# Second and third attention: GpSimd scales the softmax weights, VectorE copies the turned weights

## The chip, the cores and the metric

One core of a Trainium2 chip runs the kernel. TensorE (PE in the rows, its weight loads PEld), VectorE (DVE), ScalarE (ACT), GpSimd (POOL) and SyncE (SP) each run their own list of instructions in order, and wait for one another through semaphores. The metric is the device time of one execution in microseconds.

## The reference

The network is one block with attention over 8 heads and a convolutional feed-forward part, followed by two layers of feed-forward, attention, feed-forward. All is float32, with 256 tokens and a width of 1024. Three attentions occur. In each, per head:

```python
s = einsum(q, k) + bias            # 256 queries x 256 keys, masked to the causal part
m = max(s);  p = exp(s - m)
p = p / sum(p)                     # second attention: a learned sink joins max and sum
out = einsum(p, v)                 # 64 columns of the output per head
```

The second attention (16 heads, a window of 128, keys and values shared by four heads, a sink) and the third (16 heads, causal, a forget gate added to the logits) are the ones that the change touches. The first one (8 heads) is left as it is.

## The kernel before

**Stages.** The list `KINDS` gives eight stages in order: the first attention (`moba`), the convolutional feed-forward (`conv`), a feed-forward, the second attention (`swa`), two feed-forwards, the third attention (`fox`), a feed-forward. All weights come from memory in units of 128x2048 floats through five slots. SyncE issues the loads (L440, L452). Products are made in three passes of a cheaper format: ScalarE rounds each unit to `hi` (L629), VectorE subtracts to get `lo` (L1076), and TensorE multiplies hi by hi, lo by hi and hi by lo. `split_through(s, u)` on either engine means: do this for all units up to unit u of stage s. Where it stands in an engine's list is written out by hand.

**An attention.** The 16 heads go through a pipeline of 19 steps t = 0 to 18, again written out by hand, one loop on each engine. A head's weights are two row blocks: queries 0 to 127 against 128 keys, queries 128 to 255 against 256 keys, so 384 columns in all. There are three buffers for weights (`P_of`, by head modulo 3), two for turned weights (`PT_of`), two banks for logits, one bank at a time for the turned weights. For head h:

- TensorE, step h - 1: `logits` (L1770, L1771), two products. It waits until the maxima of head h - 2 are done.
- VectorE, step h: `max_of` (L1218, L1219) adds the bias, writes the negated logits into the weight buffer and keeps the row extreme. It waits for the logits and until head h - 3 has been turned (its buffer).
- ScalarE, step h: `exps` (L811, L812), exponentials with their sums. In the second attention it waits also for the sink value that GpSimd copies into the buffer (L538, `sinks`).
- VectorE, step h + 1: `normalise` takes the reciprocals of the two sums (L1226), then scales the two blocks (L1228, L1229).
- TensorE, step h + 2: `turn` (L1782), three transposes into a PSUM bank. It waits for the scaled weights and until the bank has been copied out for head h - 1.
- ScalarE, step h + 2: `pt_copy` (L823) copies the bank, 128x384, to SBUF. It stands behind the exponentials of head h + 2.
- TensorE, step h + 3: `values` (L1799, L1800), the product with the values. Two heads share a bank; the first of a pair waits until the pair before has been taken out.
- For each pair ScalarE makes `o_hi` (L829, step h + 3 for an odd head h) and VectorE `o_lo` (L1234, one step later). They stand at the same places in both attentions.

**What else is in the steps.** In VectorE's step the order is: `max_of(t)`, `out_lo` (odd t from 5), `normalise(t-1)`, and then work of the stage: sums and norms of query and key blocks (L1185, L1193, L1200) and `split_through`. In the second attention the splits stand at the end of steps 5, 8, 11, 13 and 15; in the third at the end of steps 0 to 3, 8, 9, 11, 13 and 17. In the third attention step 2 has, after `normalise`: sums of block 4, the split, then the norms of blocks 4 and 5. On TensorE `step_rows` (L1732 to L1734) makes the remaining query, key and value products in the early steps, before `turn`; `turn_block` (L1746) turns normed blocks, and ScalarE's `block_evict` (L783) takes them out. The logits of head 8 wait for the last of these. The output projection `step_out` (L1564 to L1566), 12 matmuls each, follows `values` in TensorE's steps 10, 13, 14 and 17, and after step 18 the rest of it runs, which waits for the last `o_lo`.

**GpSimd.** It sets pads, copies the 16 pairs of sink values in the second attention, and starts loads of modulation weights (L527). After the sinks of the second attention come the loads of the next stages. During the third attention it has no instruction: it waits for the last `values` before its next load.

Of the kernel before, what the change touches and what calls it, by code (L numbers as in the profile page):

```python
# [9 lines left out]
ALU = mybir.AluOpType  # L10
# [118 lines left out]
def build(nc, a, consts, buckets, out):  # L129
    ctx = ExitStack()  # L130
    with ctx:
# [356 lines left out]
        def _(pool):  # L488
# [21 lines left out]
            def load_pieces(stages, most=PIECES * sum(CHUNKS_IN)):  # L510
# [3 lines left out]
                while next_piece < last:  # L514
# [12 lines left out]
                    pool.dma_start(piece_of(n), ada_columns(c)[:, 2 * q:2 * q + 2, :]).then_inc(ada_full[slot], 16)  # L527
                    next_piece += 1

            def sinks(s):  # L530

                pool.wait_ge(nsink_done, 1)
                pool.wait_ge(xt_done, 4 * s + 4)
                for h in range(HEADS[KINDS[s]]):
                    n = HEAD0[s] + h
                    if n >= 3:
                        pool.wait_ge(tr_done, n - 2)
                    nc.gpsimd.tensor_copy(P_of[n % 3][:, P:P + 2 + T:T + 1],  # L538
                                          nsink[:, h:h + 1].to_broadcast([P, 2])).then_inc(sink_set, 1)

            def pad(n, ap, value):

# [70 lines left out]
            load_pieces(6)  # L613
            third_pads(6)
            forget_rows()
            load_pieces(NST)


        @block.scalar
        def _(act):  # L620
# [213 lines left out]

            def attention_outs(s, t):
                nh = HEADS[KINDS[s]]
                if 0 <= t - 2 < nh:
                    pt_copy(s, t - 2)
                if 0 <= t - 3 < nh and (t - 3) % 2:
                    out_hi(s, (t - 3) // 2)  # L840
# [176 lines left out]
        def _(dve):  # L1017
# [204 lines left out]
            def normalise(s, h):  # L1222
                n = HEAD0[s] + h
                st, pr = stat[:, n % 3, :], P_of[n % 3]
                dve.wait_ge(exp_done, n + 1)
                nc.vector.reciprocal(st[:, 4:6], st[:, 4:6]).then_inc(den_ready, 1)  # L1226
                dve.wait_ge(den_ready, n + 1)
                nc.vector.tensor_scalar(pr[:, FIRST], pr[:, FIRST], st[:, 4:5], None, ALU.mult)  # L1228
                nc.vector.tensor_scalar(pr[:, SECOND], pr[:, SECOND], st[:, 5:6], None, ALU.mult).then_inc(nm_done, 1)  # L1229

            def out_lo(s, pair):
                n = HEAD0[s] // 2 + pair
                dve.wait_ge(ohi_done, n + 1)
                nc.vector.tensor_tensor(o_lo[:, pair, :], value_bank(2 * pair), o_hi[:, pair, :].bitcast(F32),  # L1234
                                        ALU.subtract).then_inc(olo_done, 1)

            def attention_step(s, t):
                kind = KINDS[s]
# [5 lines left out]
                    out_lo(s, (t - 5) // 2)  # L1244
                if 0 <= t - 1 < nh:
                    normalise(s, t - 1)
                if t == nh + 2:
                    out_lo(s, nh // 2 - 1)

# [794 lines left out]
```

## Time and profile before

| | us |
|---|---|
| median of 3 runs (lowest, highest) | 1437.64 (1437.03, 1440.68) |
| the profiled execution | 1436.28 |
| its span in the trace | 1434.5 |

| engine | busy us | share of the span |
|---|---|---|
| TensorE, matmuls | 1357.6 | 95% |
| VectorE | 1083.2 | 76% |
| ScalarE | 730.9 | 51% |
| GpSimd | 158.4 | 11% |

The granted TensorE clock is full throughout. The second attention's head pipeline lies between about 642 and 697 us of the span, the third's between about 1144 and 1227 us. A timeline row gives start, duration, engine, line, operation, output <- inputs with shapes, and how many instructions were merged; a bracket at its end gives the idle time of the engine just before it and what ended it. Matmul ends are modelled, so starts are the better thing to subtract.

### The profile page before, as it was taken

The page shows a single profiled execution, that of the slowest core. Times are in us where ns is not written, and L with a number is a line of the kernel's source. Part 1 is how long each engine was busy: PE and PEld are TensorE (multiplying, and loading weights), DVE is VectorE, ACT ScalarE, POOL GpSimd, SP SyncE. Part 2 cuts the span into 40 slices and gives each one's busy share as a digit, 9 for nine tenths or more (in the row PEclk, how much of TensorE's full clock was granted, in tenths as well). Part 3 has the DMA queues.
Part 4 walks back from the last instruction along what each step waited for, and adds up shares of the span by engine and source line. Part 5 has one row for each costly group of instructions (what it writes and reads, how often), then busy time and mean ns, then how long its engine had stood idle before and what let it go on. Part 6 is the DMA issues. An engine that isn't in the chain of part 4 may idle for free.

```text
span 1434.5 us, 18439 instructions
## 1 busy us (share of the span) xinstructions
PE 1357.6 (95%) x7209; PEld 1154.7 (80%) x7209; DVE 1083.2 (76%) x1506; ACT 730.9 (51%) x1023; POOL 158.4 (11%) x230
## 2 busy tenths in 40 slices
PE   2899999999989999997999999999999998999998
PEld 1699988999968888786788887788887877788886
DVE  5888976999888999667678888688887656675444
ACT  3664464444564333677643345634437867743432
POOL 1111000111001221000011113011101000100000
PEclk9999999999999999999999999999999999999999
DMA  9877755888759998441588896698874531585561
GB/s 351 284 232 258 237 191 186 296 287 293 255 161 356 337 354 297 166 151 59 176 276 307 293 297 235 208 315 308 296 251 147 172 124 62 188 279 178 176 201 62
DMA packets 188794, 333.57 MB, mean 233 GB/s; under 512 B 8434, under 2 KB 131966, under 8 KB 187684
## 3 DMA queue, kind: packets, MB, share of 16 engines
q1 hardware_dynamic: 161392, 236.02, 48.9%
q0 software_dynamic: 26736, 96.14, 19.6%
q8 instruction: 58, 0.95, 0.3%
q10 hardware_dynamic: 580, 0.23, 0.1%
q14 instruction: 28, 0.23, 0.0%
HBM read 331.24 MB, written 1.12 MB: 232 GB/s over the span
## 4 chain that ended last, share of the span: by engine, by line
PE 76%; DVE 11%; ACT 6%; issue 4%; DMA 3%; SPq 0%; ACTq 0%; DVEq 0%
PE bank L1601 10%; PE bank L1603 10%; PE bank L1602 10%; PE bank L1564 8%; PE bank L1566 7%; PE bank L1565 7%; PE bank L1496 4%; PE bank L1497 4%; PE bank L1498 4%; DVE lo L1076 4%; DVE ada_sum L1034 2%; ACT hi L629 2%; PE bank L1732 2%; PE bank L1734 2%; PE bank L1733 2%
## 5 line engine op out<-in xcount | busy, mean ns | idle before, releaser
L1076 DVE TENSOR_TENSOR lo<-raw,hi 128x2048 fp32r<-128x2048 f32 x215 | 490.8, 2287 | 89.2 <-ACT hi L629 88.7
L629 ACT ACTIVATE hi<-raw 128x2048 fp32r<-128x2048 f32 x215 | 405.7, 1910 | 19.2 <-DMA raw<-in_w_out 12.3
L1601 PE MATMUL bank<-hi,h_hi 128*128 128x512 f32 x704 | 278.1, 395 | 3.6 <-DVE lo L1076 2.0
L1603 PE MATMUL bank<-hi,h_lo 128*128 128x512 f32 x704 | 274.5, 390 | 0.0
L1602 PE MATMUL bank<-lo,h_hi 128*128 128x512 f32 x704 | 274.2, 389 | 0.0
L1564 PE MATMUL bank<-hi,o_hi 128*128 128x512 f32 x504 | 203.5, 404 | 11.1 <-DVE lo L1076 9.0
L1566 PE MATMUL bank<-hi,o_lo 128*128 128x512 f32 x504 | 197.2, 391 | 0.0
L1565 PE MATMUL bank<-lo,o_hi 128*128 128x512 f32 x504 | 196.6, 390 | 0.0
L741 ACT ACTIVATE KT<-bank 128x256 f32<-128x256 f32 x88 | 33.8, 384 | 313.4 <-PE bank L1603 313.4
L1601 PEld LDWEIGHTS bank<-hi,h_hi 128*128 128x128 f32 x704 | 132.2, 188 | 33.4 <-DVE lo L1076 3.9
L1603 PEld LDWEIGHTS bank<-hi,h_lo 128*128 128x128 f32 x704 | 132.2, 188 | 28.1
L1602 PEld LDWEIGHTS bank<-lo,h_hi 128*128 128x128 f32 x704 | 132.3, 188 | 26.2
L1496 PE MATMUL bank<-h_hi,hi 128*128 128x256 f32 x480 | 137.9, 287 | 3.3 <-DVE lo L1076 3.2
L1498 PE MATMUL bank<-h_hi,lo 128*128 128x256 f32 x480 | 135.7, 283 | 0.0
L1497 PE MATMUL bank<-h_lo,hi 128*128 128x256 f32 x480 | 135.7, 283 | 0.0
L527 POOL DMA_DIRECT2D ada<-in_ada_w x100 | 71.3, 714 | 523.3 <-DVE ada_sum L1034 396.5
L1034 DVE SCALAR_TENSOR_TENSOR ada_sum<-ada,c_act,ada_sum 128x512 f32<-128x512 f32 x156 | 117.1, 750 | 8.8 <-DMA ada<-in_ada_w 2.2
L1564 PEld LDWEIGHTS bank<-hi,o_hi 128*128 128x128 f32 x504 | 94.8, 188 | 31.8 <-DVE lo L1076 12.3
L1034 DVE SCALAR_TENSOR_TENSOR ada_sum<-V,c_act,ada_sum 128x512 f32<-128x512 f32 x152 | 113.9, 749 | 3.9
L1566 PEld LDWEIGHTS bank<-hi,o_lo 128*128 128x128 f32 x504 | 94.6, 188 | 20.7
L1565 PEld LDWEIGHTS bank<-lo,o_hi 128*128 128x128 f32 x504 | 95.0, 188 | 17.4
L1165 DVE TENSOR_TENSOR KT<-KT,bank 128x256 f32<-128x256 f32 x88 | 36.2, 417 | 83.1 <-ACT KT L741 83.1
(217 smaller groups left out, 1993.9 us busy)
## 6 DMA issues: line engine op xcount, KB each, us to landing
raw<-in_ffn_w SPq DMA_DIRECT2D x176, 512.0 KB, 5.3
ada<-in_ada_w POOLq DMA_DIRECT2D x100, 512.0 KB, 5.9
raw<-in_ffn_w SPq DMA_DIRECT2D x44, 1024.0 KB, 6.3
V<-in_ada_w POOLq DMA_DIRECT2D x76, 512.0 KB, 6.1
raw<-in_w_up SPq DMA_DIRECT2D x22, 1024.0 KB, 6.4
raw<-in_w_in SPq DMA_DIRECT2D x16, 1024.0 KB, 7.9
raw<-in_fox_w_in SPq DMA_DIRECT2D x12, 1024.0 KB, 5.1
raw<-in_w_down SPq DMA_DIRECT2D x11, 1024.0 KB, 5.2
```

Source lines behind the costliest of these rows:

```text
L629: nc.scalar.activation(hi[:, n % NS, :], raw[:, n % NS, :], ACT.Copy).then_inc(hi_ready, 1)
L1034: nc.vector.scalar_tensor_tensor(acc, in0=src, scalar=c_act[:, col:col + 1], in1=acc, op0=ALU.mult, op1=ALU.add).then_inc(ada_step, 1)
L1076: nc.vector.tensor_tensor(lo[:, n % NS, :], raw[:, n % NS, :], hi[:, n % NS, :].bitcast(F32), ALU.subtract).then_inc(lo_ready, 1)
L1496: mm(outp, wh, xh, start=start, stop=False, skip_group_check=True)
L1497: mm(outp, wh, xl, start=False, stop=False, skip_group_check=True)
L1498: return mm(outp, wl, xh, start=False, stop=stop, skip_group_check=True)
L1564: mm(outp, xk_hi, wh[:, k, cut], start=start, stop=False, skip_group_check=True)
L1565: mm(outp, xk_hi, wl[:, k, cut], start=False, stop=False, skip_group_check=True)
L1566: ins = mm(outp, xk_lo, wh[:, k, cut], start=False, stop=stop, skip_group_check=True)
L1601: mm(bank[:, :], xk_hi, wh[:, i, :], start=k == 0, stop=False, skip_group_check=True)
L1602: mm(bank[:, :], xk_hi, wl[:, i, :], start=False, stop=False, skip_group_check=True)
L1603: ins = mm(bank[:, :], xk_lo, wh[:, i, :], start=False, stop=k == KD - 1, skip_group_check=True)
```

## The change

In the stages other than the first (`if s`), three things change:

- `normalise` on VectorE ends after the reciprocals. GpSimd gets a new function `weights`, which waits for them and scales the two blocks in two instructions. In the second attention it is called for head h - 1 behind the sink copy of head h; in the third for heads 0 to 15 behind `forget_rows`, before the next loads.
- ScalarE no longer copies the turned weights (`pt_copy` only for `s == 0`).
- VectorE gets `turned_weights(s, t - 2)`, at the end of its `attention_step(t)`, behind the reciprocals of head t - 1 and ahead of the block work and splits of the step. It waits for the turn of head t - 2 and for the `values` of head t - 4, then copies 128x384 from the bank.

```diff
+            def weights(s, h):
+                n = HEAD0[s] + h
+                st, pr = stat[:, n % 3, :], P_of[n % 3]
+                pool.wait_ge(den_ready, n + 1)
+                nc.gpsimd.tensor_scalar(pr[:, FIRST], pr[:, FIRST], st[:, 4:5], None, ALU.mult)
+                nc.gpsimd.tensor_scalar(pr[:, SECOND], pr[:, SECOND], st[:, 5:6], None, ALU.mult).then_inc(nm_done, 1)
...
@@ def sinks(s), in the loop over h, and behind it
+                    if h:
+                        weights(s, h - 1)
+                weights(s, HEADS[KINDS[s]] - 1)
...
             forget_rows()
+            for h in range(HEADS["fox"]):
+                weights(6, h)
             load_pieces(NST)
...
             def attention_outs(s, t):
                 nh = HEADS[KINDS[s]]
-                if 0 <= t - 2 < nh:
+                if 0 <= t - 2 < nh and s == 0:
                     pt_copy(s, t - 2)
...
                 nc.vector.reciprocal(st[:, 4:6], st[:, 4:6]).then_inc(den_ready, 1)
+                if s:
+                    return
                 dve.wait_ge(den_ready, n + 1)
...
+            def turned_weights(s, h):
+                n = HEAD0[s] + h
+                dve.wait_ge(tr_done, n + 1)
+                dve.wait_ge(pv_done, n - 1)
+                dst = PT_of[n % 2].rearrange("p (a b) -> p a b", a=3)
+                if KINDS[s] != "fox":
+                    dst = dst[:, :, ::-1]
+                nc.vector.tensor_copy(dst, turn_bank(h)[:, 0:384].rearrange("p (a b) -> p a b", a=3)).then_inc(ptc_done, 1)
...
                     normalise(s, t - 1)
+                if s and 0 <= t - 2 < nh:
+                    turned_weights(s, t - 2)
                 if t == nh + 2:
                     out_lo(s, nh // 2 - 1)
```

## Rows read from the trace of the kernel before

**Rows 1.** The page, part 1: busy us, share, instructions of each engine.

```profile
PE 1357.6 (95%) x7209; PEld 1154.7 (80%) x7209; DVE 1083.2 (76%) x1506; ACT 730.9 (51%) x1023; POOL 158.4 (11%) x230
```

**Rows 2.** Busy time by stretch: PE, PEld, DVE, ACT, POOL, clock, DMA share, GB/s.

```profile
650.00:697.30 47.30, 37.96 (x218) 31.17 (x216) 34.74 (x112) 35.50 (x88) 5.46 (x16) 1.00 0.24 76
1186.40:1227.00 40.60, 35.52 (x186) 28.92 (x187) 25.23 (x74) 27.55 (x63) 0.56 (x1) 1.00 0.24 78
```

**Rows 3.** Waits of PE, second attention: us in total, times, longest.

```profile
PE bank L1782 <- ACT work L823: 3.4, 3, 2.4
```

**Rows 4.** Waits of PE, third attention.

```profile
PE bank L1782 <- ACT work L823: 1.7, 3, 1.0
PE bank L1782 <- issue: 1.5, 1, 1.5
```

**Rows 5.** Groups of instructions, whole span: count, busy us, mean ns, idle before.

```profile
L823 ACT ACTIVATE work<-bank 128x384 f32<-128x384 f32 x40 | 19.2, 481 | 13.8 <-PE bank L1782 13.7
...
L1057 DVE TENSOR_REDUCE modc<-bank 128x4 f32<-128x512 f32 x44 | 30.1, 683 | 1.7 <-PE bank L1532 1.7
...
L1234 DVE TENSOR_TENSOR o_lo<-bank,o_hi 128x256 fp32r<-128x256 f32 x20 | 8.5, 423 | 21.6 <-ACT o_hi L829 21.5
```

**Rows 6.** GpSimd's compute instructions: duration ns min/median/max, starts, forms.

```profile
L545 POOL MEMSET VP<- x6: 317/532/536, 60.4 to 1109.9; 128x512 f32 x4, 128x256 f32 x2
L538 POOL COPY work<-nsink x16: 187/189/795, 623.1 to 685.4; 128x2 f32<-128x2 f32 x16
```

**Rows 7.** Timeline, second attention, PE.

```profile
649.87 0.49 PE L1782 MATMUL bank<-ident,work 128*128 128x128 f32 x3
...
676.43 0.49 PE L1782 MATMUL bank<-ident,work 128*128 128x128 f32 x3
...
679.95 0.52 PE L1782 MATMUL bank<-ident,work 128*128 128x128 f32 x3
680.68 0.67 PE L1799 MATMUL bank<-work,VP 128*128 128x256 f32 x2 [0.21 <-DVE o_lo L1234]
...
688.57 0.49 PE L1782 MATMUL bank<-ident,work 128*128 128x128 f32 x3
...
691.39 0.55 PE L1782 MATMUL bank<-ident,work 128*128 128x128 f32 x3 [0.47 <-DVE work L1229]
```

**Rows 8.** Timeline, second attention, DVE.

```profile
650.51 0.35 DVE L1218 CUSTOM_DVE_ANT_0 work<-bank,TB,nsink 128x128 f32<-128x128 f32 x1 [3.11 <-PE bank L1782]
...
675.44 2.29 DVE L1076 TENSOR_TENSOR lo<-raw,hi 128x2048 fp32r<-128x2048 f32 x1 [0.72 <-ACT hi L629]
677.65 0.34 DVE L1218 CUSTOM_DVE_ANT_0 work<-bank,TB,nsink 128x128 f32<-128x128 f32 x1
...
678.33 0.16 DVE L1226 RECIPROCAL stat<-stat 128x2 f32<-128x2 f32 x1
...
690.59 0.16 DVE L1226 RECIPROCAL stat<-stat 128x2 f32<-128x2 f32 x1
```

**Rows 9.** Timeline, second attention, POOL.

```profile
676.99 0.80 POOL L538 COPY work<-nsink 128x2 f32<-128x2 f32 x1 [4.21 <-PE bank L1782]
```

**Rows 10.** Timeline, third attention, PE.

```profile
1159.80 0.49 PE L1782 MATMUL bank<-ident,work 128*128 128x128 f32 x3
...
1186.37 0.46 PE L1770 MATMUL bank<-TB,q_rows 128*128 128x128 f32 x2 [1.54 <-issue]
...
1217.49 0.49 PE L1782 MATMUL bank<-ident,work 128*128 128x128 f32 x3
...
1220.83 0.52 PE L1782 MATMUL bank<-ident,work 128*128 128x128 f32 x3 [1.00 <-ACT work L823]
```

**Rows 11.** Timeline, third attention, DVE.

```profile
1162.78 0.69 DVE L1200 TENSOR_TENSOR std<-bank,hstd 128x512 f32<-128x512 f32 x1
...
1215.73 0.15 DVE L1226 RECIPROCAL stat<-stat 128x2 f32<-128x2 f32 x1
...
1216.38 0.16 DVE L1226 RECIPROCAL stat<-stat 128x2 f32<-128x2 f32 x1
```

## The prediction

> **What bounds the kernel now.** I read the page first: TensorE's matmuls fill 95% of the span, VectorE 76%, ScalarE 51% [rows 1]. Then the busy time by stretch. In the second attention from 650 us on TensorE is busy 37.96 of 47.3 us, so some 9 us are open, with VectorE at 34.74 and ScalarE at 35.50; in the third from 1186.4 on, 35.52 of 40.6, so 5 us are open [rows 2]. The change can win or lose only there. Third, the waits of TensorE: the turn (L1782) of a head waits for ScalarE's copy of the head before, three times and 3.4 us in the second attention [rows 3], three times and 1.7 us in the third, and a further turn waits 1.5 us that the view gives to no one, behind the same copy [rows 4]. Those 6.6 us are the most that moving the copy off ScalarE gives. Last, the timelines of TensorE and VectorE, step against step, which decide where the copy lands.
>
> **ScalarE's part.** It loses 32 copies of 0.48 us [rows 5], 15.4 us. It bounds no stage, so this is worth only what starts earlier behind it.
>
> **VectorE's own work.** The slot of reciprocals and two scalings is 0.65 us, from one reciprocal to the next (1215.73 to 1216.38) [rows 11]. Without the scalings and the wait for the reciprocals I leave 0.12. The copy is new here: from PSUM a reduction over 512 columns takes 0.68, a subtraction over 256 takes 0.42 [rows 5], so 384 columns take 0.55 by interpolation, 0.47 from start to start. 0.12 + 0.47 = 0.59 against 0.65: nothing won or lost. Bounds 0.42 and 0.68.
>
> **GpSimd's part.** No row shows arithmetic on this engine. Its copy of two columns takes 0.19, its memset 0.53 for 512 columns and 0.32 for 256 [rows 6], so 0.83 ns per column. Below: memset's rate for both blocks, 0.5 us. For reading and writing one after the other: 2 x 384 x 0.83 ns + 2 x 0.19 = 1.0 us. Above: twice that, 2.1. I take 1.1, near the middle row. From reciprocal to turn is 0.80 us today (690.59 to 691.39) [rows 7, 8]; less 0.5 for VectorE's scalings, plus 1.1, plus 0.1 for one more hop between engines makes 1.5 us. The Trainium skill, GPSIMD Engine Reference, "Performance versus the Vector engine", gives 1.8 cycles per element at 1.2 GHz for a tight loop; with two fixed parts of 0.19 an estimate from it is 0.96 us, and the sum below would be 0.3 us less. The same page's "Engine selection" advises VectorE for elementwise work, which speaks against the move.
>
> **The new wait, which carries the forecast.** VectorE now waits, in step t, until TensorE has turned head t - 2. Behind the waiting copy stand, in order, the step's block work, its `lo` split of 2.2 us, the next maximum and the next reciprocals. TensorE turns head t - 2 late in step t where something long precedes it. A reader of the bank starts 0.63 us after the turn starts (649.87, 650.51) [rows 7, 8]. I went through both attentions head by head; four places matter.
>
> 1. Second attention, step 11. `step_out` of step 10 holds the turn of head 9 until 676.43 [rows 7]. Today VectorE's split begins at 675.44 and the next maximum at 677.65 [rows 8]. Afterwards: 676.43 + 0.63 + 0.47 = 677.53, split until 679.74. The maximum takes 0.68 to the reciprocals (677.65 to 678.33) [rows 8], then 1.5: head 11 is turned at 681.9 where it was turned at 679.95, +2.0. The product with values behind it lay 0.73 after the turn today, waiting for `o_lo` (680.68) [rows 7], and needs only 0.33; so +1.6 reaches `step_out` of step 13 and everything behind it.
> 2. Second attention, step 15. `step_out` of step 14 holds the turn of head 13. Today VectorE's split is over at 690.59 when TensorE has just passed that turn at 688.57, and the last turn comes 2.82 us after it, at 691.39 [rows 7, 8]. Afterwards the chain is turn, 0.63, copy 0.47, split 2.2, reciprocals of head 15, 1.5: 4.8 us. +2.0. The last `step_out`s wait for this head.
> 3. Third attention, step 2. Seven products a step keep the turn of head 0 until 1159.80 [rows 10]. VectorE's order behind it is copy (until 1160.9), sums 0.6, split 2.2, norm: the norm of block 4 starts at 1164.0 and not at 1162.78 [rows 11], and TensorE's next product waits for it, +1.2. The head pipeline later waits for ScalarE's evictions: 1.54 us before the logits of head 8 (1186.37) [rows 10]. ScalarE lost five copies by then, so I cost this at 0. If that cover failed it would be +1.2.
> 4. Third attention, end. There is no split at step 15. Head 13 is turned at 1217.49, then 0.63 + 0.47, reciprocals of head 15 at 1218.6, and 1.5: 1220.1. Today the last turn is at 1220.83, because the copy before it stood behind a rounding on ScalarE [rows 10]. -0.7.
>
> The 6.6 us of waits on ScalarE's copy go, but at steps 4 to 10 what is late next is `o_lo` behind VectorE's own list, or the evictions, within 0.2 us of today's times. **Sum:** +1.6 + 2.0 + 0 - 0.7 = +2.9 us. Against the profiled execution's 1436.28 us that is 1439.2; that run is 1.36 us below the median of the runs, so the median becomes 1437.64 + 2.9 = 1440.5 us. GpSimd's bounds enter at three places (turns of heads 11 and 15, then 15): -1.8 and +3.0. So the forecast's own range is +1.1 to +5.9, 1438.7 to 1443.5.
>
> **The shared port.** Can GpSimd work beside the splits? A sink copy of two columns that takes 0.19 took 0.80 (676.99 to 677.79), and the split beside it began at 675.44 with 2.29 us, so ended at 677.73 [rows 8, 9]. GpSimd waited for the split's end. The Trainium skill, SBUF — State Buffer, "Who interferes with whom", says the pair of ports is an exclusive lock, and that whichever starts first holds it for the whole instruction. By that rule the trace agrees for GpSimd as the loser; no row shows VectorE as the loser. In the forecast GpSimd begins right after the reciprocals, while VectorE still copies, so it comes first and the split waits up to 0.6 us at steps 5 and 8 of the second attention and 9 and 11 of the third. Those delays lie before longer waits and are within the 0.2 above.
>
> **The rivals.**
> - *Locked out or slow GpSimd.* The second scaling meets a running split and ends 2.2 us later, or the two take 2.1 us. With 1.0 more at each of three places the time is +2.9 + 3.0 = +5.9; one turn behind a split (head 8 of the third attention, where today's wait of 1.5 leaves 0.9 uncovered) adds 1.3 to +2.9. I give +5, 1442.6 us. For: the 0.80 us copy. Against: the order of starts. 0.22.
> - *ScalarE's relief carries* (the other side). The roundings `hi` come up to 1 us earlier, the turns wait for no one, and VectorE's copy finds its turn done. Then of 6.6 us some 2.0 stay as new waits on `o_lo`: -4.6, 1433.0 us. It decides where TensorE has passed the turn of head t - 2 when VectorE reaches the copy. Against: at steps 11 and 15 of the second attention it has not, by 1.0 us and more. 0.10.
> - *No change.* The work moves but the losses at steps 11 and 15 are made up, because heads before them run about 2 us earlier than I have them and TensorE reaches `step_out` sooner. 1437.6 us. 0.18.
> - *The forecast*, +2.9: 0.50.
>
> **How the numbers follow.** Runs of this kernel tell a difference from none at about 0.3%, 4.3 us. Of the forecast's 0.50 about 0.36 lie within that and 0.14 above; of the locked-out case 0.05 within and 0.17 above; the relief case halves into 0.05 faster and 0.05 within; no change gives 0.18. Faster 0.05, same 0.64, slower 0.31. The range: leaving out the larger gains and the worst GpSimd gives 1434.5 to 1445.5.
>
> **What would show it.** In the changed profile: (a) VectorE's copy waits for L1782, over 2 us in all, longest at steps 11 and 15 of the second attention; (b) ScalarE falls by 15 us and VectorE stays within 3; (c) the last turn of the second attention falls 3 to 4 us after today's 691.39, the last of the third half a microsecond earlier relative to its start; (d) GpSimd's two scalings together near 1.1 us, the ones that meet a split longer; (e) the stages outside the two attentions have the same lengths. Wrong would be: no wait of VectorE on turns with a shorter second attention, or GpSimd's scalings beyond 2 us.

## The result, and the profile after

| | before | after |
|---|---|---|
| median of the runs (lowest, highest), us | 1437.61 (1437.03, 1440.68) | 1449.99 (1448.34, 1451.24) |
| span of the profiled execution | 1434.5 | 1449.4 |
| TensorE clock over the span | 0.996 | 0.987 |

The change makes the kernel slower by 12.4 us between the medians; the ratio is 1.0081 with a 95% interval of 1.0067 to 1.0096, which is 11.6 us. Four executions of the kernel after were measured, and 4 to 12 of each kernel below; ratios leave out one, of *scaling alone*, that took 7149 us. The prediction was 1440.5 us with a range up to 1445.5: right in the sign of its shift, far too small, and the time is outside the range.

The line numbers moved: the turn L1782 is L1808, `values` L1799 is L1825, the logits L1770 are L1796, `o_lo` L1234 is L1249, the split L1076 is L1089. GpSimd's scalings are L535 and L536, its sink copy L546, VectorE's copy L1259. Part 1 of the page of the kernel after, against [rows 1]:

```profile
PE 1368.2 (94%) x7209; PEld 1163.0 (80%) x7209; DVE 1080.7 (75%) x1474; ACT 719.3 (50%) x991; POOL 211.5 (15%) x294
```

VectorE has lost 2.5 us, ScalarE 11.6, GpSimd has gained 53.1. TensorE has the same instructions and is busy 10.6 us longer. That is the first sign that something other than waiting has been added.

Where the 14.9 us between the two profiled executions lie, read as start times on TensorE. A length here is the time from the first logits of an attention to the first `step_out` product behind its last head; it is used for all kernels below.

| stretch | before | after | difference |
|---|---|---|---|
| up to the first logits of the second attention | 641.74 | 642.69 | +0.95 |
| second attention | 55.52 | 65.74 | +10.22 |
| between | 446.22 | 446.21 | 0 |
| third attention | 83.40 | 87.09 | +3.69 |
| the rest of the span | 207.6 | 207.7 | +0.1 |

Busy time by stretch of the kernel after (columns as in [rows 2]), first over both attentions, then the places with a reduced clock:

```profile
641.00:700.00 59.00, 49.10 (x241) 39.66 (x240) 36.23 (x112) 33.82 (x85) 28.57 (x45) 0.88 0.15 49
700.00:712.00 12.00, 9.62 (x39) 7.97 (x40) 3.27 (x7) 4.17 (x5) 4.19 (x6) 0.86 0.58 185
1145.00:1245.00 100.00, 90.50 (x444) 74.55 (x443) 54.87 (x133) 61.62 (x115) 28.98 (x36) 0.97 0.31 106
...
660.00:670.00 10.00, 8.16 (x29) 6.42 (x28) 4.97 (x19) 5.90 (x15) 5.78 (x9) 0.50 0.00 0
671.00:677.00 6.00, 3.66 (x23) 2.86 (x22) 4.96 (x14) 1.78 (x7) 2.42 (x6) 1.00 0.00 0
686.00:692.00 6.00, 5.44 (x20) 4.52 (x21) 4.12 (x11) 3.78 (x10) 5.11 (x7) 0.72 0.00 0
700.00:706.00 6.00, 4.64 (x17) 3.97 (x18) 1.04 (x3) 1.91 (x1) 2.75 (x4) 0.72 0.70 231
```

The granted clock was 1.00 in both stretches of [rows 2]. It was not full throughout the span of the kernel before, contrary to what stands above: from 38 to 45 us and near 217 us it was at the lower level, both far from the two attentions. The second of these places:

```profile
215.00:220.00 5.00, 4.63 (x26) 4.63 (x27) 3.73 (x4) 2.82 (x4) 0.00 (x0) 0.66 0.00 0
```

In the kernel after the clock is 0.88 over the second attention: TensorE runs at the lower of its two levels, 1.2 GHz, from 660 to 670 us, near 688 and near 702, and twice in the third attention. Each time a pause of TensorE stands before the fall or around it; but the pause before 675 us, 2.3 us long and the reason for the low busy time in the row from 671 us, is followed by no fall. The waits of TensorE (as in [rows 3]) in the second attention, then VectorE's on the turn, second and third attention:

```profile
PE bank L1808 <- POOL work L536: 4.8, 4, 2.6
PE bank L1825 <- DVE o_lo L1249: 4.2, 2, 2.3
```

```profile
DVE work L1259 <- PE bank L1808: 19.8, 11, 3.6
...
DVE work L1259 <- PE bank L1808: 25.0, 12, 5.0
```

ScalarE's copy is gone from TensorE's list, as it was meant to be. In its place stand GpSimd's scaling and `o_lo`, and VectorE stands before the turn for 44.8 us in all.

The timeline of the kernel after, TensorE, at the two places of the second attention that the forecast was built on, and at the first fall of the clock:

```profile
656.17 0.55 PE L1808 MATMUL bank<-ident,work 128*128 128x128 f32 x3
658.61 0.67 PE L1825 MATMUL bank<-work,VP 128*128 128x256 f32 x2 [1.90 <-DVE o_lo L1249]
...
660.00 1.06 PE L1797 MATMUL bank<-KT,QT 128*128 128x256 f32 x2
662.03 0.90 PE L1808 MATMUL bank<-ident,work 128*128 128x128 f32 x3 [0.97 <-POOL work L536]
...
680.86 0.49 PE L1808 MATMUL bank<-ident,work 128*128 128x128 f32 x3
...
686.56 0.55 PE L1808 MATMUL bank<-ident,work 128*128 128x128 f32 x3 [0.76 <-POOL work L536]
...
696.34 0.49 PE L1808 MATMUL bank<-ident,work 128*128 128x128 f32 x3
...
701.36 0.90 PE L1808 MATMUL bank<-ident,work 128*128 128x128 f32 x3 [2.61 <-POOL work L536]
```

From the turn of head 9 to that of head 11 it is 5.70 us, where it was 3.52 [rows 7]; from head 13 to head 15, 5.02 for 2.82. A turn takes 0.5 us at the full clock and 0.90 at the lower one. The first fall lies between two pauses: TensorE has waited 1.90 us before 658.61, its products are slow from 660.00 on (1.06 us for two logits, 0.60 at the full clock), and the wait of 0.97 us that ends at 662.03 is already inside the slow stretch. VectorE and GpSimd in the same two neighbourhoods:

```profile
658.91 2.28 DVE L1089 TENSOR_TENSOR lo<-raw,hi 128x2048 fp32r<-128x2048 f32 x1
...
696.87 0.56 DVE L1259 COPY work<-bank 128x384 f32<-128x384 f32 x1 [2.12 <-PE bank L1808]
697.34 2.28 DVE L1089 TENSOR_TENSOR lo<-raw,hi 128x2048 fp32r<-128x2048 f32 x1
699.54 0.16 DVE L1239 RECIPROCAL stat<-stat 128x2 f32<-128x2 f32 x1
```

```profile
658.63 0.60 POOL L535 TENSOR_SCALAR work<-work,stat 128x128 f32<-128x128 f32 x1 [2.39 <-DVE stat L1239]
659.21 2.77 POOL L536 TENSOR_SCALAR work<-work,stat 128x256 f32<-128x256 f32 x1
...
699.79 0.60 POOL L535 TENSOR_SCALAR work<-work,stat 128x128 f32<-128x128 f32 x1 [3.43 <-DVE stat L1239]
700.37 0.93 POOL L536 TENSOR_SCALAR work<-work,stat 128x256 f32<-128x256 f32 x1
```

The chain at step 15 is link for link that of the forecast: turn, copy, split, reciprocals, scaling, turn. At 659.21 GpSimd's second scaling takes 2.77 us and not 0.93, because a split has started at 658.91; it ends 0.8 us behind that split. Over the whole span (durations in ns, least, median and most, as in [rows 6]):

```profile
L535 POOL TENSOR_SCALAR work<-work,stat x32: 596/606/610, 646.4 to 1234.2; 128x128 f32<-128x128 f32 x32
L536 POOL TENSOR_SCALAR work<-work,stat x32: 916/927/2770, 647.0 to 1234.8; 128x256 f32<-128x256 f32 x32
L546 POOL COPY work<-nsink x16: 177/188/2095, 624.1 to 693.1; 128x2 f32<-128x2 f32 x16
```

### The profile page after: what moved, and what is told of

It is laid out like the page before. It is cut to its first block, busy times and chain, and to the rows that moved or that the text cites. A ratio compares the mean times of both kernels' runs of the same rounds, so it can differ in the third digit from the quotient of the medians.

```text
span 1449.4 us, 18441 instructions
## 1 busy us (share of the span) xinstructions
PE 1368.2 (94%) x7209; PEld 1163.0 (80%) x7209; DVE 1080.7 (75%) x1474; ACT 719.3 (50%) x991; POOL 211.5 (15%) x294
## 4 chain that ended last, share of the span: by engine, by line
PE 77%; DVE 11%; ACT 4%; issue 3%; DMA 3%; POOL 1%; SPq 0%; ACTq 0%; DVEq 0%
PE bank L1627 10%; PE bank L1629 10%; PE bank L1628 10%; PE bank L1590 8%; PE bank L1592 8%; PE bank L1591 8%; PE bank L1522 4%; PE bank L1523 4%; PE bank L1524 4%; DVE lo L1089 3%; DVE ada_sum L1047 2%; PE bank L1758 2%; PE bank L1760 2%; PE bank L1759 2%; PE bank L1638 1%
## 5 line engine op out<-in xcount | busy, mean ns | idle before, releaser
L1089 DVE TENSOR_TENSOR lo<-raw,hi 128x2048 fp32r<-128x2048 f32 x215 | 490.8, 2286 | 82.4 <-ACT hi L642 82.1
L527 POOL DMA_DIRECT2D V<-in_ada_w x76 | 54.6, 719 | 369.6 <-DVE ada_sum L1047 364.4
```

What stands on the lines that cost most here:

```text
L1089: nc.vector.tensor_tensor(lo[:, n % NS, :], raw[:, n % NS, :], hi[:, n % NS, :].bitcast(F32), ALU.subtract).then_inc(lo_ready, 1)
```

## The experiments

Theory A: VectorE's wait for the turn, in order ahead of its block work and splits, carries the loss. Theory B: GpSimd does, by its latency and its lock-outs. Theory C: the pauses take TensorE's clock to 1.2 GHz, and that multiplies whatever A or B cost. Where a cost is given "by the ratio", it is the ratio's distance from 1 times the median before. Ratios are to the kernel before, run in the same rounds; its median over those runs was 1438.4 to 1438.6, and 1437.61 beside the kernel after. The lengths and clocks are those of one profiled execution each.

| kernel | median us | ratio (95%) | second | third | clock, span |
|---|---|---|---|---|---|
| before | 1438.55 | | 55.52 | 83.40 | 0.996 |
| after | 1449.99 | 1.0081 (1.0067, 1.0096) | 65.74 | 87.09 | 0.987 |
| copy alone | 1445.41 | 1.0057 (1.0039, 1.0075) | 61.10 | 85.14 | 0.992 |
| scaling alone | 1439.25 | 1.0007 (0.9997, 1.0018) | 56.99 | 83.40 | 0.993 |
| copy last | 1439.49 | 1.0011 (1.0000, 1.0022) | 57.18 | 82.98 | 0.997 |
| splits wait | 1445.72 | 1.0059 (1.0040, 1.0078) | 62.17 | 85.00 | 0.991 |
| fillers | 1445.37 | 1.0055 (1.0034, 1.0077) | 60.55 | 85.55 | 0.999 |
| copy last, VectorE scales | 1440.53 | 1.0015 (1.0003, 1.0026) | 58.05 | 82.16 | 0.998 |
| two splits ahead | 1445.35 | 1.0045 (1.0032, 1.0057) | 57.38 | 85.46 | 0.996 |
| outs first | 1438.18 | 1.0001 (0.9988, 1.0014) | 56.21 | 83.45 | 0.996 |
| before with fillers | 1439.53 | 1.0011 (1.0002, 1.0020) | 57.54 | 83.63 | 0.998 |
| third alone | 1439.83 | 1.0015 (1.0003, 1.0028) | 56.18 | 85.44 | 0.996 |
| third, copy last, VectorE scales | 1436.57 | 0.9987 (0.9977, 0.9997) | 55.53 | 82.21 | 0.998 |
| six places late | 1443.75 | 1.0037 (1.0022, 1.0051) | 62.01 | 83.70 | 0.990 |

**Each half by itself.** *Copy alone*: VectorE scales as before and copies as in the change.

```diff
@@ normalise, against the kernel after
-                if s:
-                    return
@@ sinks, and behind forget_rows: the calls of weights are gone
```

> Only the copy is moved: VectorE scales as before and copies the turned weights at the place of the change; ScalarE has no copy, GpSimd no scaling. The whole change costs +12.4 us. Theory A (VectorE's in-order wait for the turn carries the loss): +3 to +6 us. Theory B (GpSimd's latency of 1.53 us between reciprocal and turn, and its lock-out by the splits, carry it): -1 to +2 us. Theory C (TensorE's pauses drop its clock, and the clock carries most of it): no long pause of TensorE is left here, so the granted clock of the second attention is back near 1.00 and the time within 2 us of A's or B's.

*Scaling alone*: GpSimd scales, ScalarE copies.

```diff
@@ attention_outs on ScalarE, against the kernel after
-                if 0 <= t - 2 < nh and s == 0:
+                if 0 <= t - 2 < nh:
@@ attention_step on VectorE
-                if s and 0 <= t - 2 < nh:
-                    turned_weights(s, t - 2)
```

> Only the scaling is moved: GpSimd scales, ScalarE copies the turned weights as before. Theory A: +1 to +3 us, since no engine waits for a turn ahead of a split. Theory B: +7 to +11 us. Theory C: the loss follows the granted clock of the second attention (0.88 in the changed kernel): if it stays under 0.93 the loss is over +5 us, if it is above 0.98 under +3 us.

By the ratios the copy alone costs 8.2 us (7.0 by the medians), more than A expected (+3 to +6), and the scaling alone 1.0, at the low end of it. B falls: its +7 to +11 for the scaling does not come, and GpSimd's extra latency lengthens the second attention by 1.5 us and the third not at all. The two halves add up to 9.2 us of the 11.6 by the ratios, a difference that the intervals leave open; the lengths of the two attentions, one profiled execution each, add up to 8.8 of 13.9. C's expectation for the copy alone, no long pause and a clock near 1.00, failed. TensorE waits there 2.38 and 2.46 us for `o_lo`, and its clock falls twice in the second attention, so these 8 us hold a share of the clock as well:

```profile
642.36:703.46 61.10, 49.74 (x257) 41.04 (x256) 45.85 (x147) 34.85 (x87) 6.40 (x16) 0.94 0.21 69
```

**The same copy at another place.** *Copy last*: the whole change, but each step of VectorE ends with the copy, behind the block work and the split.

```diff
@@ attention_step on VectorE, against the kernel after
-                if s and 0 <= t - 2 < nh:
-                    turned_weights(s, t - 2)
@@ the loops of the second and the third attention, last in the step
+                        if 0 <= t - 2 < HEADS[kind]:
+                            turned_weights(s, t - 2)
```

> The whole change, but VectorE's copy stands at the very end of each step, behind the block work and the split of the step. A split no longer waits for a turn. Theory A: the copies are later by a split in five steps, but the splits and maxima are back; +6 to +9 us instead of +12.4. Theory B: nothing gained, +11 to +14 us, since GpSimd then starts beside the split at every split and is locked out five times in each attention.

Ten of the 11.6 us go by the ratios, 11.3 of the 12.4 by the medians, more than both theories expected, with the same instructions on every engine. Waits of VectorE on the turn in that kernel, second and third attention:

```profile
DVE work L1259 <- PE bank L1810: 7.5, 6, 3.6
...
DVE work L1259 <- PE bank L1810: 9.7, 7, 3.2
```

19.8 and 25.0 us have become 7.5 and 9.7, and what is left has no split behind it in its own step. So the order in VectorE's list is the cause. That the copy runs on VectorE is not. The clock stayed full in this kernel's second attention, so what the order and what the clock gave back come together here. GpSimd's scaling was locked out by a split three times in it (2.56, 2.66 and 2.56 us for 0.60), against twice in the kernel after, so the lock-outs by themselves cannot carry the loss:

```profile
L535 POOL TENSOR_SCALAR work<-work,stat x32: 594/603/2658, 647.1 to 1222.4; 128x128 f32<-128x128 f32 x32
```

**The lock-outs.** *Splits wait*: the whole change, and a split of an attention step starts only when the scaling of that step is done.

```diff
@@ the loop of the second attention on VectorE; in the third likewise
                         if t in (5, 8, 11, 13, 15):
+                            dve.wait_ge(nm_done, HEAD0[s] + t)
                             split_through(s, 6 + (5, 8, 11, 13, 15).index(t))
```

> The whole change, and before each split of steps 5, 8, 11, 13, 15 (second attention) and 8, 9, 11, 13, 17 (third) VectorE also waits until GpSimd has scaled, so no scaling is locked out. The two lock-outs of 1.84 us (a scaling of 2.77 instead of 0.93) go, each split there is up to 1.3 us later. Theory A: no change, +11 to +13.5 us. Theory B with the lock as its main part: +8 to +10 us, and the clock of the second attention above 0.92.

4.3 us come back by the medians and 3.2 by the ratios, whose intervals overlap with those of the kernel after. The loss left is 8.5 us by the ratio, as the lock theory expected, and 7.3 by the medians, a little under it. In the second attention head 4 is turned 17.75 us after the first logits, and 19.34 in the kernel after, where its scaling takes 2.77. TensorE's clock falls here too, at other places (1.00 from 660 to 670 us, 0.83 from 670 to 680), so the time of this run does not separate lock-out and clock. The traces do in part. *Two splits ahead*, below, has the lock-out and a full clock, and this kernel's clock is full as well until just before the turn of head 8. Head 4 is turned at 19.35 us there and at 17.75 here, but head 5 at 22.59 and 23.19, and head 8 at 30.45 and 31.68. In the second attention, then, the lock-out costs nothing that lasts to head 5, and making the split wait costs 1.2 us by head 8; what this run wins over the kernel after comes with a shorter and later fall of the clock. In the third attention the lock-out does cost: head 8 is turned at 57.26 us here, although the clock has just fallen, and at 58.47 with the change in the third alone, at the full clock.

**The clock by itself.** *Fillers*: the whole change, nothing taken away, and 43 products of the identity with itself whose output nothing reads, where the kernel after pauses.

```diff
@@ TensorE, against the kernel after
+            FILL_TURN = {("swa", 4): 4, ("swa", 15): 10, ("swa", 11): 3, ("fox", 11): 3}
+            FILL_VALUES = {("swa", 2): 7, ("swa", 6): 8, ("fox", 8): 8}
+            def filler(bank, count):
+                for _ in range(count):
+                    mm(bank[:, 0:P], ident[:, :], ident[:, :], start=True, stop=True)
@@ turn and values: filler(...) behind the wait for ptc_done, ahead of the wait for nm_done or olo_done
```

> The changed kernel with products of the identity with itself put where its trace has TensorE waiting over half a microsecond: in the second attention before the values of heads 2 and 6 and the turns of heads 4, 11 and 15, in the third before the values of head 8 and the turn of head 11; 43 products that nothing reads, in banks that are free there. Work is added and nothing taken away, no edge between engines is changed. Theory C (the pauses drop TensorE's clock to 1.2 GHz and that multiplies the loss): the granted clock of the second attention goes back from 0.88 to over 0.97, and the time falls although there is more to do: the stretches at half speed in the changed kernel cost some 7 us in the second attention and 3.5 in the third by their busy time, of which I expect 4 to 8 us back, so 1442 to 1446. Rival (the clock is a bystander): the time stays at 1449 to 1452 or rises with each filler that overshoots its pause, whatever the clock does.

```profile
641.00:700.00 59.00, 53.33 (x321) 45.25 (x319) 37.24 (x114) 35.31 (x86) 32.76 (x48) 1.00 0.21 65
700.00:712.00 12.00, 10.98 (x50) 8.96 (x49) 5.45 (x7) 5.86 (x12) 1.44 (x2) 1.00 0.52 177
1145.00:1245.00 100.00, 91.02 (x476) 76.19 (x474) 57.00 (x133) 60.99 (x119) 28.89 (x36) 1.00 0.36 122
```

The clock is 1.00 throughout (same stretches as above), and the kernel is faster for doing more, by 4.6 us between the medians and 3.7 between the ratios (four executions each; the two intervals overlap by 0.001). One filler group overshoots, as TensorE's and GpSimd's rows at step 15 show (a product of the identity counts as two instructions):

```profile
696.01 2.50 PE L1805 MATMUL bank<-ident 128*128 128x128 f32 x20 [1.52 <-DVE work L1259]
698.35 0.49 PE L1817 MATMUL bank<-ident,work 128*128 128x128 f32 x3
```

```profile
696.18 0.92 POOL L536 TENSOR_SCALAR work<-work,stat 128x256 f32<-128x256 f32 x1
```

The scaling ends at 697.10, the turn starts at 698.35: about 1.2 us too many. *Before with fillers* is the control: the same 43 products in the kernel before.

> Control of the run with fillers: the kernel before with the same 43 products of the identity at the same seven places. Its clock is at full speed there and its pauses lie elsewhere, so there is nothing to win back. Theory C (fillers helped the changed kernel only by its clock): slower than the kernel before, by +2 to +8 us (43 products of 0.25 us are 10.8 us, part of which falls in pauses that exist here too). Rival (filler products shorten something by themselves): 1438 or less.

It is 1.0 us slower by the medians and 1.6 by the ratio. That is less than the 2 I expected at least, since more of the products fall in pauses than I had counted; but they win nothing where the clock is full. Theory C holds; the two kernels compared at the end of the next part say the same without fillers.

**Which places.** *Two splits ahead*: only the two steps that the forecast charged.

```diff
@@ attention_step on VectorE, against the kernel after
+                if kind == "swa" and t in (11, 15):
+                    split_through(s, 6 + (5, 8, 11, 13, 15).index(t))
                 if s and 0 <= t - 2 < nh:
                     turned_weights(s, t - 2)
```

> The changed kernel with the splits of steps 11 and 15 of the second attention put ahead of the copy, all other steps as in the change. These are the two places that the prediction charged, 1.6 and 2.0 us. Theory A as predicted (these two places hold the whole loss): 1438 to 1440. Theory A widened (the in-order wait costs at every step that has a split, and each pause is doubled by the clock): the turns of the changed kernel are already 5.7 us late at head 11, so only the later half comes back, 4 to 6 us: 1444 to 1446.

*Third alone*: the change only where `KINDS[s] == "fox"`.

> The change in the third attention alone; the second is as in the kernel before. The third attention took 3.7 us longer in the changed kernel, 2.15 with its clock at full speed in the run with fillers. Theory A with C: +2 to +4 us in all, 1440.5 to 1442.5, with the stall at the turned block of step 2 (1.0 us) in the trace. Rival (the loss in the third is carried over from the second): within 1 us of the kernel before.

2.2 us by the ratio, 1.3 by the medians, a little under what I expected; the third attention takes 85.44 us, +2.0, and the stall at the turned block is there with 1.02. The loss in the third is its own and not carried over. The second attention of this kernel is that of the kernel before, instruction for instruction, and the clock fell in it all the same, from 658.8 to 662.2 us: it took 56.18 us for 55.52. The stretch from 655 to 665 us:

```profile
655.00:665.00 10.00, 6.91 (x35) 5.88 (x36) 7.97 (x27) 7.32 (x25) 0.40 (x3) 0.83 0.00 0
```

*Six places late*: the copy stands behind block work and split at six steps.

```diff
@@ against the kernel after
+            LATE = {"moba": (), "swa": (11, 15), "fox": (2, 4, 9, 11)}
-                if s and 0 <= t - 2 < nh:
+                if s and 0 <= t - 2 < nh and t not in LATE[kind]:
                     turned_weights(s, t - 2)
@@ the loops of the second and the third attention, last in the step
+                        if t in LATE[kind]:
+                            turned_weights(s, t - 2)
```

> The changed kernel with VectorE's copy moved behind the block work and the splits at six of its 38 steps only: steps 11 and 15 of the second attention, steps 2, 4, 9 and 11 of the third. Theory A with places: these six carry nearly all of the loss, so the second attention takes 57 to 58 us (55.5 before, 65.7 after), the third 83 to 84 (83.4 and 87.1), and the whole is +1.5 to +4 us, 1440 to 1442. Rival (the wait at every step adds up): over 1445.

The whole is +5.3 us by the ratio, above the 1.5 to 4 expected and under the rival's 1445. In the third attention the six-places kernel is back at 83.70, from 85.44 with the change in the third alone, but that does not show that the loss sat at steps 2, 4, 9 and 11. Head 5 is turned at 44.91 us, 46.34 with the change in the third alone, so the later copies of steps 2 and 4 give back 1.4 us. The pauses of TensorE before the `values` of head 6 and the turn of head 8 stay, 2.19 and 1.99 us, because the copy of step 8 still stands ahead of its split. In the second, *two splits ahead* and *six places late* have the same order on every engine, yet one took 57.38 us and the other 62.01. Busy time from 10 to 20 and from 20 to 30 us after the first logits, first of *two splits ahead*, then of *six places late*:

```profile
656.54:666.54 10.00, 6.24 (x39) 4.68 (x38) 8.71 (x26) 7.20 (x20) 7.32 (x11) 1.00 0.30 100
666.54:676.54 10.00, 6.84 (x44) 5.63 (x43) 8.12 (x27) 6.61 (x19) 7.04 (x10) 1.00 0.00 0
```

```profile
652.45:662.45 10.00, 6.77 (x37) 4.91 (x36) 8.64 (x25) 7.20 (x20) 7.32 (x11) 0.86 0.29 97
662.45:672.45 10.00, 8.95 (x39) 7.37 (x37) 4.82 (x15) 5.63 (x15) 4.35 (x8) 0.63 0.00 0
```

VectorE, ScalarE and GpSimd do the same in the first of the two stretches, to 0.07 us. TensorE's clock is full in one kernel and falls in the other, and by the turn of head 10 that has cost 3.25 us (36.82 and 40.07 us after the first logits). The expectation for the second attention (57 to 58) failed by this alone. The median of *two splits ahead* lies where the widened theory A put it, but not for its reason: of the 10.2 us in the second attention 8.4 came back, and nearly 5 us of its profiled execution were lost ahead of that attention (first logits at 646.54). They are lost within the first 157 us, where no kernel here differs from another; in the 14 profiled executions the first logits of the second attention lie between 641.15 and 646.54 us. What moves them is open.

**Versions that might be better.** *Copy last, VectorE scales* gives the scaling back to VectorE.

> VectorE scales the weights as in the kernel before and also copies the turned weights, but the copy is the last thing of each step, behind the block work and the splits; GpSimd has no scaling and ScalarE no copy in the second and third attention. Theory A (what costs is the place of the copy ahead of the splits, not that VectorE copies): the loss of 7 us of the run with the copy alone is gone, 1436.0 to 1438.5. Rival B (VectorE has too much to do with both): 1440 to 1443.

The third attention gains (82.16), the second loses (58.05): TensorE there waits 1.8, 1.8 and 1.4 us for VectorE, before the turns of heads 3, 7 and 14, whose predecessors' copies now end steps 4, 8 and 15. So the expectation of A failed here and B's held: with both jobs VectorE is late at these three steps. The clock fell here too, from 660.8 to 664.2 us, so not all of the 2.5 us in the second attention is VectorE's. *Outs first* leaves the kernel before as it is, except for ScalarE's order in step 4 of the second attention.

```diff
@@ the loop of the second attention on ScalarE, against the kernel before
+                        if t == 4:
+                            attention_outs(s, t)
                         attention_exps(s, t)
                         if t == 2:
                             block_square(s, 5)
-                        attention_outs(s, t)
+                        if t != 4:
+                            attention_outs(s, t)
```

> The kernel before with one edit on ScalarE: in step 4 of the second attention the copy of head 2 and the first o_hi come ahead of the exponentials, whose table load (1.28 us at 654.31) and run they now wait behind. The turn of head 3 waits 2.44 us for this copy in the kernel before. If ScalarE's order at this one step is what the change could have relieved: turn of head 3 at 13.5 us after the first logits instead of 15.4, and 0.5 to 1.5 us of the span, 1436 to 1437.5. Rival (the exponentials of head 4 come half a microsecond later and the next turns wait for them): no change, 1437.5 to 1438.5.

```profile
654.23 0.52 PE L1785 MATMUL bank<-ident,work 128*128 128x128 f32 x3
656.80 0.67 PE L1802 MATMUL bank<-work,VP 128*128 128x256 f32 x2 [2.05 <-DVE o_lo L1237]
```

The turn of head 3 comes at 13.1 us and not at 15.4, and TensorE's very next product waits 2.05 us for `o_lo`. It starts at 15.65 us and not at 16.10, and by head 5 nothing is left of that (22.92 us, 22.61 before). The time is that of the kernel before, as the rival said. So next to nothing of the largest wait on ScalarE's copy, 2.4 of the 3.4 us in [rows 3], was to be had. The clock fell later in this attention, from 662.8 to 666.2 us, so its whole length is no clean comparison. *Third, copy last, VectorE scales* keeps what won:

```diff
@@ against the kernel before: ScalarE
-                if 0 <= t - 2 < nh:
+                if 0 <= t - 2 < nh and KINDS[s] != "fox":
@@ the loop of the third attention on VectorE, last in the step
+                        if 0 <= t - 2 < HEADS[kind]:
+                            turned_weights(s, t - 2)
```

> A version that may beat the kernel before: second attention as before; in the third VectorE scales as before and takes over the copy as the last thing of each step, ScalarE has no copy, GpSimd no scaling. With the same order in both attentions the third took 82.16 us against 83.40 in the kernel before. Expected: 1.2 us less, 1436.5 to 1437.8. Rival (one profiled run of the third attention does not carry over, or the splits it leaves later cost it elsewhere): within 0.5 us of the kernel before.

Its ratio of 0.9987, with an interval of 0.9977 to 0.9997, is the only one below 1: 1436.57 us, 2.0 below the kernel before by the medians, of which the third attention explains 1.2. Twelve variants were run and the interval ends just under 1, so this is a hint of a gain and no more. Its second attention takes 55.53 us, as before. It takes from the change the move of the copy, where ScalarE's order had held it up, and leaves the rest.

## Why the prediction was wrong, point by point

**Right, with its numbers.** Place 1, step 11 of the second attention: forecast 5.5 us from the turn of head 9 to that of head 11, measured 5.70. Place 2, step 15: forecast 4.8 from turn to turn, measured 5.02. VectorE neither gained nor lost (1080.7 busy against 1083.2), and its slot from reciprocals to the end of the copy is 0.53 (699.54 to `o_lo` at 700.07), forecast 0.59. GpSimd's two scalings take 0.606 + 0.927 = 1.53 us and not 1.1, within the bounds; from reciprocals to turn it is 1.82 (699.54 to 701.36) and not 1.5. Place 3: the stall of TensorE at the turned block in the third attention came, 1.0 us of the 1.2, and its cover held: in the run of the third alone head 5 is turned 46.34 us after the first logits, and 46.37 in the kernel before. Place 4: from the turn of head 13 to that of head 15 in the third, 2.81 us in that run for 3.34 before, -0.5 of the -0.7. Stages outside the two attentions kept their lengths to 0.1 us, but for the 0.95 ahead of the second, which is within the scatter of that start in the profiled executions.

**Its signs.** VectorE waits for turns 44.8 us in all, not just over 2, and longest for heads 0 and 5 of the second attention (3.6 and 3.1 us) and head 0 of the third (5.0), not at steps 11 and 15. ScalarE's busy time falls by 11.6 us and not by 15: the copies took 15.4, but partly beside its other instructions. The last turn of the second attention comes 10 us after 691.39, not 3 to 4, and the last of the third 3.8 us later from its start (81.15 for 77.36), not half a microsecond earlier. One slip of the working: with 0.96 for the scalings the sum would be 0.4 us less, three times 0.14, not 0.3.

**The step that failed: the sum had no term for TensorE's clock.** I costed every product at its duration before, as if a pause cost only itself. With the clock held up by fillers the second attention takes 60.55 us, about 59.3 without the 1.2 us of overshoot: +3.8 against the +3.6 of places 1 and 2. "At steps 4 to 10 within 0.2 us of today's times" holds in that run for heads 5, 6, 8, 9 and 10, though not for head 4 (19.29 us, 17.93 before): head 10 is turned 36.53 us after the first logits, 36.33 before. In the kernel after it is 39.82. By this estimate the clock adds the other 6.4 of the 10.2 us (65.74 - 59.3) in the second attention and 1.5 of the 3.7 (87.09 - 85.55) in the third: some 8 of the 14.9 us between the profiled executions. These are single executions; between the medians the fillers gave back 4.6 of the 12.4 us, near 6 with the overshoot. The pause of 1.90 us on `o_lo` at step 5 was small, and at the full clock it is made up by head 5 (turned at 22.53 us with fillers and 22.59 in *two splits ahead*, 22.61 before). In the kernel after, ten microseconds at 1.2 GHz begin 1.4 us behind it, and head 5 is turned at 24.66.

**A place that was missed: steps 8 and 9 of the third attention.** I charged the third with -0.7; at the full clock it is +2.0 (85.44). VectorE, GpSimd and TensorE in the kernel with the change in the third alone:

```profile
1195.31 0.56 DVE L1256 COPY work<-bank 128x384 f32<-128x384 f32 x1 [3.20 <-PE bank L1805]
1195.79 2.28 DVE L1086 TENSOR_TENSOR lo<-raw,hi 128x2048 fp32r<-128x2048 f32 x1
...
1198.54 0.42 DVE L1246 TENSOR_TENSOR o_lo<-bank,o_hi 128x256 fp32r<-128x256 f32 x1
...
1199.40 2.28 DVE L1086 TENSOR_TENSOR lo<-raw,hi 128x2048 fp32r<-128x2048 f32 x1
```

```profile
1199.70 2.77 POOL L536 TENSOR_SCALAR work<-work,stat 128x256 f32<-128x256 f32 x1
```

```profile
1194.78 0.49 PE L1805 MATMUL bank<-ident,work 128*128 128x128 f32 x3
...
1199.10 0.67 PE L1822 MATMUL bank<-work,VP 128*128 128x256 f32 x2 [2.19 <-DVE o_lo L1246]
...
1202.53 0.55 PE L1805 MATMUL bank<-ident,work 128*128 128x128 f32 x3 [1.87 <-POOL work L536]
```

The copy of step 8 waits 3.20 us for the turn of head 6, which the products of `step_rows` hold until 1194.78. The split of step 8 starts only then, the next maximum and `o_lo` behind it, and TensorE's `values` wait 2.19 us. Then the split of step 9 locks GpSimd out, and the turn of head 8 waits 1.87 more. This is the mechanism of places 1 and 2, and it delays two of TensorE's products; I had looked for it only where a `step_out` holds the turn, and at step 2. It costs 2.5 us at head 8 (58.47 for 55.99 us after the first logits), 2.0 of which last to the end.

**The order of starts.** "It comes first, and the split waits": the opposite happened. VectorE's copy is over before GpSimd's first scaling is, so the split starts in the middle of it, at 658.91, and the second scaling starts at 659.21 and ends at 661.98, 0.8 us behind the split and 1.84 us late. The splits of this kernel took 2.28 us as ever. I should have compared 0.47 us of copy with 0.6 of the first scaling. The Trainium skill, SBUF — State Buffer, "Who interferes with whom", has the pair of ports go to whoever issues first, for the whole instruction. The trace agrees for L536, which took 2.77 beside a split that had started 0.3 us before it; but L535 and the split that starts 0.3 us ahead of its end show no delay in their durations. Where a split starts earlier in a scaling, VectorE does lose a little, as in *two splits ahead*, first GpSimd, then VectorE:

```profile
671.64 0.93 POOL L536 TENSOR_SCALAR work<-work,stat 128x256 f32<-128x256 f32 x1
```

```profile
671.77 2.48 DVE L1089 TENSOR_TENSOR lo<-raw,hi 128x2048 fp32r<-128x2048 f32 x1
```

The split takes 2.48 us for 2.28, although 0.80 us of the scaling were left. I gave this rival 0.22 and 1442.6 us. The lock-outs are real: they cost 1.2 us at head 8 of the third attention, nothing that lasts at step 5 of the second, and they are far from the whole of the loss.

**What stays open.** What makes the clock fall after one pause and not after another. The kernel before has pauses of 2.44 and 2.36 us within 9 us, and its clock stays at 1.00; in *third alone*, with the same instructions and the same 2.44 us, it fell. *Two splits ahead* and *six places late*, which share another order of this attention, went different ways too. The Trainium skill, TensorE: Matmul & The Clock Gate, "The HAM clock gate", has a gate that looks at TensorE's activity on a count of its own, which does not start with the kernel; by that the same pauses can cost much or nothing, as in these kernels. No run here moved the pauses against that count on purpose. The clock over the span is 0.987 to 0.992 in all four executions of the kernel after and 0.990 to 0.999 in the 29 of the kernel before beside the last runs, so in the kernel after the falls are not rare.

## What to carry to other kernels

Before moving work to another engine, ask what stands behind it in that engine's list: the same instructions cost 12 us ahead of the splits and 1 to 2 behind them. A wait that an instruction removes is worth only the distance to the next release; *outs first* won its 2.3 us at the turn and gave nearly all of them back at the next product. And price a new pause of TensorE at more than its length where TensorE is the bound: between two kernels with the same order and the same pause of 1.90 us, the stretch at 1.2 GHz behind it cost 3.25 us, and a few products that nobody reads, put into the pause, show whether it did.

## What the runs showed of the hardware that was not expected

- A pause of 1.90 us was followed, 1.4 us after its end, by 10 us at a granted clock of 0.50; in another kernel the same pause was followed by none. Products in this and six other pauses kept the clock at 1.00, and the kernel was 4.6 us faster by the medians with them.
- GpSimd scales 128 columns by a value per row in 0.606 us and 256 in 0.927: 2.5 ns for each further column and about 0.29 fixed.
- A GpSimd instruction that starts 0.2 to 0.3 us into a split of VectorE is held up by it: a scaling took 2.77 us for 0.93 and ended 0.8 us behind the split, a copy of two columns 2.10 for 0.19 and ended with it.
- A split that starts 0.13 us into a scaling of GpSimd took 2.48 us for 2.28, while the scaling kept its 0.93.
